# Twelve TensorE bodies for the expert widths in place of six

## The chip, the cores and the metric

One core of one Trainium2 chip runs the whole program in one launch. The metric is the device time of one execution in microseconds (us); three runs of the kernel before are given.

## The reference

One decoder layer on 1024 tokens of width 1024, all in f32: a mixer of latent attention and forgetting attention, a cross attention over 256 memory tokens, a mixture of 32 experts, and a last norm. Only the experts matter here:

```python
logits = (xt @ w_router).astype(jnp.float32) + b_router.astype(jnp.float32)
top_vals, top_idx = lax.top_k(logits, TOP_K)          # TOP_K = 4
gates = jax.nn.softmax(top_vals, axis=-1)
...
h = lax.ragged_dot(xs, w_gate_up, group_sizes) + b_gate_up[e_sorted]
glu = jnp.minimum(h[:, ::2], SWIGLU_LIMIT)
lin = jnp.clip(h[:, 1::2], -SWIGLU_LIMIT, SWIGLU_LIMIT)
act = glu * jax.nn.sigmoid(SWIGLU_ALPHA * glu) * (lin + 1.0)
y = lax.ragged_dot(act, w_down, group_sizes) + b_down[e_sorted]
```

Each token goes to 4 of the 32 experts, 4096 rows in all. The reference's router, worked out on its own inputs, gives the experts these numbers of tokens, largest first: 199, 195, 180, 171, 156, 152, 145, 143, 140, 138, 135, 131, 130, and then nineteen experts of 125 down to 78.

## The kernel before

The program runs its stages one after the other: memory keys and values, the input projections, attention, cross attention and router, and from about 1070 us on the experts. Every engine has its own instruction stream; semaphores tie them together.

**The router's end.** The vector engine counts the tokens of each expert, ranks the experts by size, largest first (`order`, `ahead_of`, `at_place`), and compares each expert's size with a row of widths (`widths`, filled by one memset for each width at L2231, compared at L2262 into `over_b`). A product with ones (L1724) turns that into `bounds`: how many experts are larger than 208, than 184, and so on. `items` holds, in rank order, the expert and its number of tokens.

**One item is one expert.** SyncE loads its weights into six slots of 2 MB (four of `w_gate_up`, two of `w_down`), GpSimd gathers its tokens' rows into `xg`, TensorE transposes them into `xe_t` (with VectorE), makes gate and up (`e_gate_up`: 128 products of 128x128 weights with w columns, L1376), VectorE and ScalarE make the activation over all 256 columns whatever w is, and TensorE makes the down product (`down`: 64 products with w columns, L1804). An f32 product stands in the trace as two matmul records, so an item has 256 records of L1376 and 128 of L1804. In between TensorE does parts of its neighbours: the index product and the gathered rows of the next item, and the rows of the item before on their way out. The body for w = 128 is another one: its down product takes the activations as weights (`e_rows_down`, L1836).

**The width is in the code, not in a register.** For each width from the largest down TensorE has a body of its own, inside five nested loops of two rounds; each level asks first whether the item counter `at` is still below the class's bound:

```python
def up_to(end, w, level):                 # L1914
    with pe.Fori(0, 2):                   # L1916
        with pe.If_lt(at, end):           # L1917
            if level == 1:
                item(w)
            else:
                up_to(end, w, level - 1)

for c, w in enumerate(reversed(WIDTHS)):  # L1923
    up_to(below[c], w, LEVELS)            # LEVELS = 5
```

The bounds are read into registers one by one ahead of that (`pe.value_load(bounds[...])`, L1886), the first three before `e_index(0)`, which makes the first item's gather indices, the others behind it; then come the transposes of the bias rows (L1892). A class whose bound is equal to the one before it is empty: TensorE asks at the outermost level, jumps over the body, goes round once more, and jumps over it again. Where a class ends in the middle of its loops, each level not yet finished asks once more and is refused. The other engines have one body for all widths, so nothing in their order depends on the class. Behind the classes stands one more body, for experts beyond 256 tokens (`further_blocks`, tested at L552), which this input does not use.

Of the kernel before, what the change touches and what calls it, by code (L numbers as in the profile page):

```python
# [30 lines left out]
P = 128  # L31
# [22 lines left out]
def shapes(x, mem, w_q_up, w_router, w_in):  # L54

    class S:
        pass

    S.T, S.D = x.shape[1:]
    S.NT, S.KD = S.T // P, S.D // P  # L60
    S.M = mem.shape[1]
    S.MT = S.M // P
    S.QR, S.KR, S.RO = 256, 128, 32
    S.H, S.DN, S.DV = 8, 64, 64
    S.DQ = S.DN + S.RO
    S.FW = S.H * S.DV
    S.LAT = S.QR + S.KR + S.RO + S.H
    S.IN = S.LAT + 3 * S.FW
    S.XH, S.XD = 4, S.D // 4
    S.E = w_router.shape[-1]  # L70
    S.TOP = 4
    S.CAP = 256
    S.MORE = S.T * S.TOP // (S.CAP + 1)
    S.ITEMS = S.E + S.MORE
    S.CLASSES = 6
    return S


def build(nc, S, a, out):
    T, D, NT, KD, H, FW, E, CAP = S.T, S.D, S.NT, S.KD, S.H, S.FW, S.E, S.CAP  # L80
    ctx = ExitStack()
    with ctx:
# [182 lines left out]
        widths = r("widths", [P, S.CLASSES - 1])  # L265
        over_b = r("over_b", [P, S.CLASSES - 1], BF16)

        WIDTHS = [P, 144, 160, 184, 208, CAP]
        assert len(WIDTHS) == S.CLASSES
        SLOTS = 6  # L270
        slots = [Region(95 + 16 * c, 111 + 16 * c)(f"slot{c}", [P, KD, 512]) for c in range(SLOTS)]
# [1093 lines left out]
        def _(pe):  # L1365
# [548 lines left out]
# [10 lines that stand above are left out]
                up_to(below[c], w, LEVELS)  # L1924
# [10 lines left out]
        def _(ve):  # L1935
# [294 lines left out]
            for c in range(S.CLASSES - 1):  # L2230
                ve.memset(widths[:, c:c + 1], float(WIDTHS[S.CLASSES - 2 - c]))  # L2231
            ve.wait_ge(c_rstd, 2)
# [295 lines left out]
```

## Time and profile before

| | us |
|---|---|
| runs | 2705.48, 2710.2, 2710.97; median 2710.2 |
| profiled execution, from its first to its last instruction | 2705.4 |
| experts, from the first gate product to TensorE's last | 1090.6 to 2689.2 |
| items at 208, 184, 160, 144, 128 columns | 2, 2, 3, 6, 19 |

The profile gives the span of its execution and no time of that execution beside it; the fastest run is 0.1 us above the span, the median 4.8 us. On the page an engine's share of busy time is one line, below it the span in 40 slices. "PE" is TensorE's matmul side, "PEld" its weight load, "PEldq" TensorE's sequencer, which handles loops, branches and register loads and hands matmuls to the engine's queue; its instructions are not counted as busy time, but a query by source line shows them.

### The profile page before, as it was taken

What the parts mean: (1) busy time and instruction counts of PE and PEld (TensorE: products, weight loads), DVE (VectorE), ACT (ScalarE), POOL (GpSimd) and SP (SyncE); (2) the same over time, 40 slices, a digit from 0 to 9 for tenths busy, and PEclk for the clock granted to TensorE, in tenths of its full rate; (3) what the DMA queues carried; (4) which work ended last, traced back from release to release, by engine and by line L of the source; (5) the groups of instructions that cost most, each with busy time, mean ns of one, the idle gap of its engine ahead of it and who ended that gap; (6) DMA issues with size and microseconds to landing.
All of it is one profiled execution on the core that took longest, in us unless ns stands there. A gap on an engine that the chain in (4) does not pass through costs nothing.

```text
span 2705.4 us, 49571 instructions
## 1 busy us (share of the span) xinstructions
PE 2638.0 (98%) x17206; PEld 2118.7 (78%) x17207; DVE 1091.5 (40%) x2701; ACT 627.4 (23%) x1386; POOL 379.9 (14%) x391
## 2 busy tenths in 40 slices
PE   9999999999999998999999999999999999999997
PEld 8455556666477774999999999998878787878785
DVE  1111145554212324433333344344455454545455
ACT  0333355553011112011111111111212121221212
POOL 0100022221000001111111111111111111112111
PEclk9999999999999998999999999999999999999998
DMA  8111243232300002765667677787888888888885
GB/s 293 47 51 54 64 151 90 79 116 92 129 1 9 31 31 103 303 209 194 221 218 254 225 276 260 269 274 264 318 299 319 301 310 306 312 297 312 300 310 202
DMA packets 108856, 533.95 MB, mean 197 GB/s; under 512 B 24290, under 2 KB 59042, under 8 KB 84208
## 3 DMA queue, kind: packets, MB, share of 16 engines
q1 hardware_dynamic: 88016, 498.99, 50.2%
q0 software_dynamic: 20768, 33.97, 5.7%
q8 instruction: 48, 0.79, 0.1%
q14 instruction: 24, 0.20, 0.0%
HBM read 506.64 MB, written 60.52 MB: 210 GB/s over the span
## 4 chain that ended last, share of the span: by engine, by line
PE 92%; DVE 3%; issue 2%; DMA 2%; ACT 1%; DVEq 1%; POOL 0%; ACTq 0%; POOLq 0%
PE bank L1376 45%; PE wide L1376 9%; PE wide L1836 9%; PE wide L1804 9%; PE bank L1426 8%; PE bank L1369 4%; PE wide L1500 2%; PE bank L1556 2%; PE bank L1760 2%; PE wide L1517 1%; DMA d_sum<-y_sb,sidx 1%; PE wide L1369 1%; DVE biased L2060 1%; DVE prob_t L2071 1%; ACT prob L1151 0%
## 5 line engine op out<-in xcount | busy, mean ns | idle before, releaser
L1376 PE MATMUL bank<-xe_t,slot 128*128 128x128 f32 (+4 forms) x8192 | 1025.2, 287 | 12.3 <-issue 11.2
L1376 PEld LDWEIGHTS bank<-xe_t,slot 128*128 128x128 f32 x8192 | 1014.5, 192 | 14.1 <-issue 13.7
L2336 DVE TENSOR_SCALAR glu<-bank,b_gu 128x256 f32<-128x256 f32 x256 | 123.8, 484 | 657.2 <-PE bank L1376 657.1
L1317 ACT ACTIVATE sig<-glu 128x256 f32<-128x256 f32 x256 | 106.7, 417 | 837.8 <-DVE glu L2336 835.5
L1836 PE MATMUL wide<-slot,act_t 128*128 128x512 f32 x608 | 267.8, 593 | 1.0 <-DVE act_t L2348 1.0
L1804 PE MATMUL wide<-act_t,slot 128*128 128x144 f32 (+3 forms) x1664 | 235.5, 302 | 0.0
L1804 PEld LDWEIGHTS wide<-act_t,slot 128*128 128x128 f32 x1664 | 231.8, 190 | 0.0
L1426 PE MATMUL bank<-w_in,xt 128*128 128x512 f32 (+1 forms) x512 | 217.6, 575 | 1.6 <-DVEq L1978 1.6
L1836 PEld LDWEIGHTS wide<-slot,act_t 128*128 128x128 f32 x608 | 112.5, 190 | 128.8 <-issue 126.2
L1334 ACT ACTIVATE y_t<-wide,b_dn 128x256 f32<-128x256 f32 x248 | 102.0, 471 | 421.2 <-PE wide L1836 212.9
L955 POOL DMA_INDIRECT xg<-d_xn,gidx x66 | 66.6, 1009 | 862.8 <-DVE gidx L2290 814.0
L1426 PEld LDWEIGHTS bank<-w_in,xt 128*128 128x128 f32 x512 | 94.8, 190 | 100.5 <-issue 100.5
L987 POOL DMA_INDIRECT share<-d_gate,sidx x64 | 67.8, 1059 | 458.6 <-DVEq L2357 415.4
L2348 DVE TENSOR_TENSOR act_t<-lin,sig 128x256 f32<-128x256 f32 x256 | 108.8, 425 | 41.0 <-issue 7.3
L1938 DVE TENSOR_TENSOR xe_t<-bank,gains 128x512 f32<-128x512 f32 x132 | 85.2, 686 | 96.8 <-PE bank L1760 91.6
L2338 DVE TENSOR_SCALAR lin<-bank,b_gu 128x256 f32<-128x256 f32 x256 | 121.6, 475 | 0.0
L2345 DVE TENSOR_TENSOR lin<-lin,glu 128x256 f32<-128x256 f32 x256 | 108.9, 425 | 19.4 <-issue 0.3
L1376 PEld LDWEIGHTS bank<-hn_t,w_xq 128*128 128x128 f32 x1024 | 115.5, 192 | 1.4 <-issue 1.1
L1376 PE MATMUL bank<-hn_t,w_xq 128*128 128x128 f32 x1024 | 115.7, 275 | 0.3 <-issue 0.3
L1376 PE MATMUL wide<-vw,px_t 128*128 128x512 f32 x256 | 112.4, 593 | 0.6 <-DVE lg_now L2171 0.6
L997 POOL DMA_INDIRECT d_sum<-y_sb,sidx x62 | 99.0, 1598 | 44.3 <-ACTq L1299 29.4
L1369 PE MATMUL bank<-const,prob 128*128 128x128 f32 x576 | 88.2, 281 | 11.6 <-DVE prob_t L2071 5.1
(302 smaller groups left out, 2455.6 us busy)
## 6 DMA issues: line engine op xcount, KB each, us to landing
slot<-in_w_gu SPq DMA_DIRECT2D x128, 2048.0 KB, 8.8
slot<-in_w_dn SPq DMA_DIRECT2D x64, 2048.0 KB, 7.7
w_in<-in_w_in SPq DMA_DIRECT2D x1, 6144.0 KB, 25.3
w_mem_k<-in_w_mem_kv SPq DMA_DIRECT2D x4, 1024.0 KB, 11.0
w_mem_v<-in_w_mem_kv SPq DMA_DIRECT2D x1, 4096.0 KB, 20.6
x_sb<-in_x SPq DMA_DIRECT2D x8, 512.0 KB, 3.3
cneg<-d_cneg SPq DMA_DIRECT2D x8, 512.0 KB, 6.6
d_vw<-mix_out SPq DMA_DIRECT2D x16, 256.0 KB, 2.2
```

The source lines that it names most:

```text
L997: po.indirect_dma_start(out=d_sum, out_offset=bass.IndirectOffsetOnAxis(ap=sidx[:, hb:hb + 1], axis=0), in_=y_sb[:, hb, :], in_offset=None ...
L1317: ac.activation(sig[m % 2][:, :], glu[m % 2][:, :], ACT.Sigmoid, scale=1.702).then_inc(e_sig, 1)
L1334: x = ac.activation(y_t[:, m, :], pp2[b][:, (m % 2) * CAP:(m % 2 + 1) * CAP], ACT.Identity, bias=b_dn[:, bass.ds(e * KD + m, 1)])
L1369: m = pe.transpose(dst[0:s.shape[-1], j * P:j * P + s.shape[0]], s, idn)
L1376: m = pe.matmul(dst, l, r_, start=(k == 0), stop=(k == n - 1))
L1426: m = pe.matmul(pp[b][:, 0:c1 - c0], xt[:, kk, :], w_in[:, kk, c0:c1], start=kk == 0, stop=kk == KD - 1)
L1804: x = pe.matmul(pp2[b][:, (m % 2) * CAP:(m % 2) * CAP + w], slots[4 + m // 4][:, k, (m % 4) * P:(m % 4 + 1) * P], act_t[:, k, 0:w], start= ...
L1836: x = pe.matmul(wide[1][:, hd * 512:(hd + 1) * 512], act_t[:, k, 0:P], slots[4 + hd][:, k, :], start=k == 0, stop=False)
L2336: ve.tensor_scalar(glu[b][:, :], pp[b][:, 0:CAP], b_gu[:, bass.ds(e * 2 * KD + 2 * m, 1)], 7.0, ALU.add, ALU.min).then_inc(e_glu, 1)
L2338: ve.tensor_scalar(lin[b][:, :], pp[b][:, CAP:2 * CAP], b_gu[:, bass.ds(e * 2 * KD + 2 * m + 1, 1)], 7.0, ALU.add, ALU.min).then_inc(e_gu[ ...
L2345: ve.tensor_tensor(lin[b][:, :], lin[b][:, :], glu[b][:, :], ALU.mult)
L2348: ve.tensor_tensor(act_t[:, m, :], lin[b][:, :], sig[b][:, :], ALU.mult).then_inc(e_act, 1)
```

## The change

The table of widths becomes every eighth number from 128 to 208, and 256: twelve classes and twelve bodies instead of six. Everything that depends on the number of classes follows: eleven memsets of `widths`, eleven columns in `over_b` and in its product, eleven bounds and eleven register loads. What a body does is unchanged.

```diff
@@ -72,7 +72,8 @@
     S.CAP = 256
     S.MORE = S.T * S.TOP // (S.CAP + 1)
     S.ITEMS = S.E + S.MORE
-    S.CLASSES = 6
+    S.STEP = 8
+    S.CLASSES = (208 - P) // S.STEP + 2
     return S
@@ -265,7 +266,7 @@
         widths = r("widths", [P, S.CLASSES - 1])
         over_b = r("over_b", [P, S.CLASSES - 1], BF16)
 
-        WIDTHS = [P, 144, 160, 184, 208, CAP]
+        WIDTHS = [*range(P, 208 + S.STEP, S.STEP), CAP]
         assert len(WIDTHS) == S.CLASSES
```

One line is added ahead of the bodies, so a line of TensorE's code has a number higher by one in the changed kernel (L1377 for L1376).

With the sizes above the experts fall into these classes:

| tokens | 199, 195 | 180 | 171 | 156 | 152 | 145 | 143, 140, 138 | 135, 131, 130 | the other 19 |
|---|---|---|---|---|---|---|---|---|---|
| width before | 208 | 184 | 184 | 160 | 160 | 160 | 144 | 144 | 128 |
| width after | 200 | 184 | 176 | 160 | 152 | 152 | 144 | 136 | 128 |

Summed over the 32 experts the columns fall from 4560 to 4496. Before, one class is empty (256). After, four are: 256, 208, 192 and 168.

TensorE, ahead of the first item. Before, from the first item's index product on (`mv`, `hot`) to the first test of class 256:

```order
L1376 MATMUL bank<-mv,hot 128x2 x16
L1886 TENSOR_LOAD bounds
L1886 ISA x2
...
L1892 MATMUL wide<-const,b_thrice 96x128 x8
L1916 UNCONDITIONAL_BRANCH
L1917 COMPARE_AND_BRANCH
```

and in the changed kernel:

```order
L1377 MATMUL bank<-mv,hot 128x2 x16
L1887 TENSOR_LOAD bounds
L1887 ISA x2
...
L1893 MATMUL wide<-const,b_thrice 96x128 x8
L1917 UNCONDITIONAL_BRANCH
L1918 COMPARE_AND_BRANCH
```

The load and its two further instructions stand twice before and eight times after between the index product and the bias rows; ahead of the index product they stand three times in both.

TensorE, the way from the last product of the body for 184 columns to the first of the next body, before:

```order
L1804 MATMUL wide<-act_t,slot_189 128x184 x16
L1917 UNCONDITIONAL_BRANCH
L1916 REGISTER_ALU
L1916 COMPARE_AND_BRANCH
...
L1909 COMPARE_AND_BRANCH
L1760 MATMUL bank<-const,xg 128x128 x16
...
L1376 MATMUL bank<-xe_t,slot_184 128x160 x16
```

and in the changed kernel the way from the body for 176 columns to the one that follows in the code:

```order
L1805 MATMUL wide<-act_t,slot_189 128x176 x16
L1918 UNCONDITIONAL_BRANCH
L1917 REGISTER_ALU
L1917 COMPARE_AND_BRANCH
...
L1910 COMPARE_AND_BRANCH
L1761 MATMUL bank<-const,xg 128x128 x16
...
L1377 MATMUL bank<-xe_t,slot_184 128x168 x16
```

The loop's ends and heads are the same (five of each), but what follows the body for 176 is a whole body for 168 columns, which no expert of this input enters, and only behind that the one for 160.

## Rows read from the trace of the kernel before

**Rows 1.** The page: span and busy time of the engines.
```profile
span 2705.4 us, 49571 instructions
PE 2638.0 (98%) x17206; PEld 2118.7 (78%) x17207; DVE 1091.5 (40%) x2701; ACT 627.4 (23%) x1386; POOL 379.9 (14%) x391
```

**Rows 2.** Groups by shape, L1376: line engine op, count | busy us, mean ns | idle before.
```profile
L1376 PE MATMUL bank<-xe_t,slot 128*128 128x128 f32 x4864 | 551.0, 275 | 2.7 <-issue 2.7
L1376 PE MATMUL bank<-xe_t,slot 128*128 128x144 f32 x1536 | 193.0, 288 | 3.3 <-issue 3.3
L1376 PE MATMUL bank<-xe_t,slot 128*128 128x160 f32 x768 | 105.9, 299 | 2.9 <-issue 2.9
L1376 PE MATMUL bank<-xe_t,slot 128*128 128x208 f32 x512 | 92.7, 344 | 1.0 <-DVEq L2305 1.0
L1376 PE MATMUL bank<-xe_t,slot 128*128 128x184 f32 x512 | 82.5, 324 | 2.4 <-issue 2.4
```

**Rows 3.** Timeline of TensorE: start, us, what, count, idle time before it.
```profile
1216.71 17.05 PE L1804 MATMUL wide<-act_t,slot 128*128 128x208 f32 x96
1236.15 11.91 PE L1376 MATMUL bank<-xe_t,slot 128*128 128x184 f32 x64 [2.39 <-issue]
...
1301.71 10.14 PE L1376 MATMUL bank<-xe_t,slot 128*128 128x184 f32 x64
...
1350.53 15.12 PE L1804 MATMUL wide<-act_t,slot 128*128 128x184 f32 x96
1368.52 8.96 PE L1376 MATMUL bank<-xe_t,slot 128*128 128x160 f32 x64 [2.87 <-issue]
...
1424.72 8.86 PE L1376 MATMUL bank<-xe_t,slot 128*128 128x160 f32 x64
...
1540.37 9.78 PE L1376 MATMUL bank<-xe_t,slot 128*128 128x144 f32 x64 [3.28 <-issue]
...
1593.13 8.00 PE L1376 MATMUL bank<-xe_t,slot 128*128 128x144 f32 x64
...
1850.02 7.41 PE L1376 MATMUL bank<-xe_t,slot 128*128 128x128 f32 x64 [2.70 <-issue]
```

**Rows 4.** TensorE's sequencer by source line: count: ns min/median/max, first and last start.
```profile
L1917 PEldq COMPARE_BRANCH  x92: 65/73/4747, 1078.5 to 2685.5; - x92
...
L1886 PEldq TENSOR_LOAD <-bounds x5: 295/306/309, 1074.8 to 1077.5; - x5
...
L552 PEldq COMPARE_BRANCH  x1: 4821/4821/4821, 2687.2 to 2687.2; - x1
```

**Rows 5.** The same by window: 1078 to 1084.3 (two rows), then 1231 to 1234.
```profile
L1917 PEldq COMPARE_BRANCH  x2: 221/2484/4747, 1078.5 to 1083.7; - x2
...
L1916 PEldq MOVE  x2: 35/36/38, 1078.4 to 1084.3; - x2
...
L1917 PEldq COMPARE_BRANCH  x4: 214/214/222, 1231.1 to 1233.8; - x4
```

**Rows 6.** The chain that ended last, 1080 to 1086: start, us, what.
```profile
1080.68 4.70 DMA xg<-d_xn,gidx
1085.37 0.39 issue
```

**Rows 7.** Windows: PE, PEld, DVE, ACT, POOL busy (count); PEclk, DMA share, GB/s.
```profile
1090.00:1094.00 4.00, 3.39 (x10) 3.31 (x11) 3.14 (x4) 0.00 (x0) 3.39 (x3) 0.50 1.00 426
1238.00:1242.00 4.00, 4.00 (x19) 4.00 (x18) 0.00 (x0) 0.00 (x0) 0.00 (x0) 0.65 0.77 328
1366.00:1372.00 6.00, 3.48 (x25) 3.49 (x26) 0.00 (x0) 0.63 (x2) 0.00 (x0) 1.00 0.82 298
```

**Rows 8.** DMA packets that fetch instructions, 1236 to 1540, then 1855 to 2680: count, MB, share.
```profile
q8 instruction: 7, 0.11, 0.2%
...
q8 instruction: 2, 0.03, 0.0%
```

## The prediction

> **What bounds the kernel now.** I read the page first, then the groups by shape, then TensorE's timeline over the experts, and last its sequencer, because the change adds nothing but code. The page shows TensorE's matmuls busy for 98% of the span and every other engine below half of it [rows 1]. So what counts is TensorE's time for an item, and whether it gets its next item at once.
>
> Per matmul record, the groups give 551.0/4864 = 0.113 us at 128 columns, 0.126 at 144, 0.138 at 160, 0.161 at 184 and 0.181 at 208 [rows 2]: the time follows the columns. Of 32 groups' starts only five have idle time ahead of them in these rows. One is the very first item, behind VectorE. The other four stand exactly where the width changes: 2.39, 2.87, 3.28 and 2.70 us, and what they wait for is "issue", that is, nothing that another engine owes [rows 2, 3]. Between two items of one width there is no gap. A change of width is therefore a cost of its own, 11.24 us in all, and the change makes more of them.
>
> There is a second cost behind it. The first 64 gate records after a change took 11.91 us at 184 columns, against 10.14 one item later; 9.78 against 8.00 at 144; but 8.96 against 8.86 at 160 [rows 3]. The granted clock says why: 0.65 in the four microseconds after the gap at 1236, which is a part at the lower level, 1.2 GHz, after an engine that had stood idle for 2.39 us; 1.00 around the gap of 2.87 us at 1368 [rows 7]. So two of four gaps brought the lower clock, at 1.77 us each.
>
> **What the sequencer shows.** The tests of line 1917 take 65 to 73 ns in the median and once 4747 ns [rows 4]. That one, at 1078.5, is the first jump over the body for 256 columns, which is empty. The second jump over the same body, on the loop's second round, took 221 ns [rows 5]. At the end of a class, four refused tests jump over a body that has just run, in 214 to 222 ns each [rows 5]. The jump over the last, unused body at the program's end took 4821 ns [rows 4]. So it is not the jump that is dear, and not its length, but landing in code that was not reached before. Instruction packets fit: seven of 16 KB while the classes of 184 and 160 made their first passes, and two in 825 us of the 128-column items [rows 8]. Seven packets for two bodies is about 56 KB for a body, and a body once run is kept. The Trainium skill, page "Runtime: NRT & Kernel Launch", section "Instruction fetch mechanics", says that a taken branch to a target outside what is held forces a fetch before execution goes on; it gives no time for it. By that rule the trace's two long branches are fetches; the trace agrees, and the time is the trace's.
>
> **The change, part by part.**
>
> *Fewer columns.* 4560 becomes 4496, 64 less. A down group of 96 records takes 17.05 us at 208 and 15.12 at 184 [rows 3]: 1.93/24 = 0.0804 us per column, times four for the 384 records of an item = 0.322 us per column and item. 64 x 0.322 = **-20.6 us**. No expert moves to or from the special body for 128 (the smallest above 128 has 130), so nothing else is saved. All of it lies on the path: TensorE has no gaps inside items. VectorE and ScalarE work on 256 columns in both and are under half busy. An item of 136 columns is still longer than one of 128, and those run without waiting for weights [rows 2], so weights don't become the bound.
>
> *Six more register loads.* Five loads start from 1074.8 to 1077.5 [rows 4], 0.68 us apart: six more take 4.1 us. What could cover them is the first item's gather. It lands at 1080.68 + 4.70 = 1085.38, and the transposes start 0.38 later [rows 6]. But the sequencer is no earlier: its walk through the empty class ends with the MOVE at 1084.3 [rows 5], and behind that stand the inner loop heads, four pairs of some 0.2 us and the two tests of the item, until about 1085.6. There is no slack left, so all of it is on the path: **+4.1 us**. If the gather were still the later one by half a microsecond, it would be 3.6; that is the low end. The bias rows behind the loads are used only at 128 columns, hundreds of microseconds later.
>
> *The empty class 208, ahead of the first item.* An empty class costs from one outer MOVE to the next, 1078.4 to 1084.3 [rows 5]: 5.9 us, of which 4.75 is the first jump. Before, one stands there (256), now two: **+5.9 us**. Low end: 1.1 us, if the target's code were already there. High end: the trace has only 4747 and 4821 ns, each once, so I allow half as much again, 7 us for the jump.
>
> *Changes of width.* Before, four. Now seven: 200 to 184 (across the empty 192), 184 to 176, 176 to 160 (across the empty 168), 160 to 152, 152 to 144, 144 to 136, 136 to 128. A gap has two parts that differ. Each level that isn't finished asks once more: after six items three times (gap 2.70), after two or three items four times (2.39 to 3.28), so after one item five times. The 144 class (three refusals, 2.70) against the 160 class (four, 3.28) makes a refusal 0.6 us. And the narrower the class that ends, the less work waits in TensorE's queue to cover it: 2.39 after 208, 2.87 after 184, 3.28 after 160, at four refusals each. So: 184 to 176, 2.87 + 0.6 = 3.5; 160 to 152, 3.28 + 0.6 = 3.9; 152 to 144, 3.3; 144 to 136, 3.4; 136 to 128, 3.5. The two across an empty class take 5.9 more: 200 to 184, 2.5 + 5.9 = 8.4; 176 to 160, 2.9 + 0.6 + 5.9 = 9.4. Sum 35.4, less the 11.2 of before: **+24.2 us**. Low end 14.7 (jumps already fetched), high end 28.
>
> *The clock.* Two of four gaps up to 3.28 us brought the lower clock. All seven are now 3.3 us or more. I take both long ones and four of the five short ones: 6 x 1.77 = 10.6, less 3.5 of before: **+7.1 us**. Bounds: -3.5 (no drop at all) and +12.4 (each of seven, the long ones for twice as long, since after the long idle ahead of the first item the clock was 0.50 for the whole stretch from 1090 to 1094 [rows 7]). The Trainium skill's page "TensorE: Matmul & The Clock Gate", section "HAM oscillation", says that the loss is paid again at every idle stretch that is long enough; by that rule all seven lose it, 12.4 in place of 10.6, and the sum would be 1.8 higher.
>
> *The rest.* Six memsets of `widths` and six more columns in one compare and one product come to under half a microsecond; the memsets stand in front of a wait of VectorE for the next stage, which covers them. If they were not covered, 0.4 us.
>
> Sum: -20.6 + 4.1 + 5.9 + 24.2 + 7.1 = **+20.7 us** on the profiled execution's span of 2705.4 us, so 2726.1. That execution is at the low end of the runs, whose median is 4.8 us above it; against the median it is 2710.2 + 20.7 = 2730.9, rounded to **2731**.
>
> **The rivals.** A measurement of this kernel can tell 0.2%, 5.4 us, from no change.
>
> *A. The forecast*, 2731, its own range 2722 to 2740 by the bounds above. Chance 0.70.
>
> *B. Empty bodies cost no fetch.* The three new empty classes are crossed at 1.1 us each instead of 5.9, say because short classes leave the fetcher ahead. 3 x 4.8 = 14.4 less: 2716.5. For it: one of the jumps of before was into cold code right after another stage, so it may have been dear for that. Against it: the 4821 ns at the end. The page "Advanced Engine Details and Errata" of the Trainium skill, section "Control Flow Timing", gives about 108 ns for a compare-and-branch, which agrees with the 65 to 222 ns here but not with the two long ones; by it alone B would hold. Chance 0.12, just above the 0.2% in half of it.
>
> *C. The columns win.* B's cheap jumps, and the clock stays up at the gaps, since it did at 2.87 us. Then -20.6 + 4.1 + 1.1 + 14.7 - 3.5 = -4.2, and if the gather covers the start after all, -9.4: 2701. It decides where all that is added stays under 15.2 us (20.6 - 5.4). Nothing in the rows gives both at once. Chance 0.05.
>
> *D. Thin classes fall behind the fetcher.* Three classes now hold a single item, so their body runs once and the next one must have been fetched during that pass; before, each had two passes or more. If entering after a single pass stalls for 4.75 us, three of these add 14: 2745. For it: bodies are kept only after a first pass. Against it: the packets of a first pass come during that pass, with 50 us to spare. Chance 0.11.
>
> *E. Nothing is done.* The classes might not be chosen as I counted (a size off by a few tokens); then some of the terms shrink together. Chance 0.02, about no change.
>
> Faster 0.05 (C). Within 0.2%: part of B and E, 0.07. Slower 0.88. The range from 2715 to 2743 takes in A with its bounds and B, and leaves out C, D and E.
>
> **What would show it.** In the changed profile: matmul groups at 200, 176, 152 and 136 columns with 512, 256, 512 and 768 records of L1377, and none at 208; on line 1918 four branches of 4 us or more (before the first item two, two among the items) where there was one; seven gaps "issue" ahead of L1377, two of them above 8 us; the first gate product some 10 us later than 1090.6; the clock below 1.00 behind most gaps; and the 128-column items as long as before, 44 us. The prediction is wrong if the crossings of 192 and 168 show branches of 0.2 us (then B), if entries after single items show long branches (D), or if the first gate product starts where it did.

## The result, and the profile after

The changed kernel takes 2743.4 us (median of four runs, 2739.1 to 2746.1) against 2709.1 of before: a ratio of 1.0128, 95% interval 1.0113 to 1.0142. It is slower, as forecast, but by 34 us where 21 were forecast, and lies just outside the range. One execution of this study, of the kernel with nine widths in nested loops, took 5527.5 us, twice as long as any other; it counts in that kernel's median and not in its ratio.

The groups by shape (columns as in [rows 2]) show that the table of widths does what it says: records at 200, 176, 152 and 136 columns in the numbers foretold, and none at 208.

```profile
L1377 PE MATMUL bank<-xe_t,slot 128*128 128x128 f32 x4864 | 552.7, 276 | 3.8 <-issue 3.8
L1377 PE MATMUL bank<-xe_t,slot 128*128 128x144 f32 x768 | 97.3, 289 | 3.2 <-issue 3.2
L1377 PE MATMUL bank<-xe_t,slot 128*128 128x136 f32 x768 | 92.1, 282 | 3.4 <-issue 3.4
L1377 PE MATMUL bank<-xe_t,slot 128*128 128x200 f32 x512 | 89.3, 337 | 1.0 <-DVEq L2306 1.0
L1377 PE MATMUL bank<-xe_t,slot 128*128 128x152 f32 x512 | 68.9, 297 | 3.8 <-issue 3.8
L1377 PE MATMUL bank<-xe_t,slot 128*128 128x184 f32 x256 | 42.2, 328 | 12.0 <-issue 12.0
L1377 PE MATMUL bank<-xe_t,slot 128*128 128x176 f32 x256 | 41.7, 328 | 3.4 <-issue 3.4
L1377 PE MATMUL bank<-xe_t,slot 128*128 128x160 f32 x256 | 38.0, 313 | 18.2 <-issue 18.2
```

The idle times put down to "issue" at the rows' ends are the seven gaps. TensorE's timeline (as [rows 3]) has them in order of time, with the first group after each:

```profile
1224.86 16.41 PE L1805 MATMUL wide<-act_t,slot 128*128 128x200 f32 x96
1253.29 11.93 PE L1377 MATMUL bank<-xe_t,slot 128*128 128x184 f32 x64 [12.03 <-issue]
...
1322.45 12.74 PE L1377 MATMUL bank<-xe_t,slot 128*128 128x176 f32 x64 [3.42 <-issue]
...
1405.07 11.54 PE L1377 MATMUL bank<-xe_t,slot 128*128 128x160 f32 x64 [18.20 <-issue]
...
1523.10 8.43 PE L1377 MATMUL bank<-xe_t,slot 128*128 128x152 f32 x64
1580.05 9.77 PE L1377 MATMUL bank<-xe_t,slot 128*128 128x144 f32 x64 [3.24 <-issue]
```

Among the items TensorE stands idle 47.9 us, in seven gaps, where it stood 11.2. The five direct changes of width cost 3.2 to 3.8 us each, the two across an empty class 12.0 and 18.2. The sequencer's branches of line 1918 (line 1917 before, [rows 4, 5]), in windows around 1083.7, 1089.2, 1242.4, 1388.6 and 1395.5 us, say what happens there:

```profile
L1918 PEldq COMPARE_BRANCH  x1: 4484/4484/4484, 1083.7 to 1083.7; - x1
...
L1918 PEldq COMPARE_BRANCH  x1: 6619/6619/6619, 1089.2 to 1089.2; - x1
...
L1918 PEldq COMPARE_BRANCH  x1: 7190/7190/7190, 1242.4 to 1242.4; - x1
...
L1918 PEldq COMPARE_BRANCH  x1: 6176/6176/6176, 1388.6 to 1388.6; - x1
...
L1918 PEldq COMPARE_BRANCH  x1: 7384/7384/7384, 1395.5 to 1395.5; - x1
```

In order these are the jumps over 256, 208, 192, 168 and, the one that nobody had on the list, 168 once more, on the loop's second round. At the other empty classes the second jump took 0.22 us. In the trace of the changed kernel every one of the five has an instruction packet of queue q8 that starts 2.3 to 2.5 us before the branch ends. A shorter stall stands on line 1910 ahead of the item of 184, 1.1 us.

The chain that ended last shows the start (as [rows 6]): the gather lands at 1081.80 + 5.04 and the transposes start 11.53 us later, where 0.39 stood before.

```profile
1081.80 5.04 DMA xg<-d_xn,gidx
1086.83 11.53 issue
```

And the clock over 20 us around the longest gap (as [rows 7]) is at the lower level (0.50, which is 1.2 GHz) throughout, with TensorE idle for most of it:

```profile
1390.00:1410.00 20.00, 4.93 (x18) 4.94 (x19) 0.00 (x0) 0.00 (x0) 0.00 (x0) 0.50 0.23 90
```

**Where 38.9 us went**, from span 2705.4 to span 2744.3 (the profiled execution of the changed kernel is its slowest, 2746.1 us, so this is 4 to 5 us more than the medians differ by). The start is taken from the first item's index product to its first gate product (13.8 us before, 25.1 after); the clock is each first group of 64 records less the same group one item later, or, where there is one item, less 64 records at the pace of the width.

| term | forecast | measured |
|---|---|---|
| 64 columns less | -20.6 | -20.6 |
| start: six loads and the crossing of 208 | +10.0 | +11.3 |
| gaps among the items | +24.2 | 47.86 - 11.24 = +36.6 |
| clock behind them | +7.1 | 14.4 - 3.8 = +10.6 |
| before the experts | 0 | +1.3 |
| sum | +20.7 | +39.2 |

The sum is 0.3 us above the difference of the spans. The 1.3 us ahead of the experts come and go from run to run: the first index product starts between 1076.7 and 1080.4 us in the profiles of this study.

### The profile page after: what moved, and what is told of

Same layout as the page of the kernel before. It is cut to its first block, busy times and chain, and to the rows that moved or that the text cites. A ratio compares the mean times of both kernels' runs of the same rounds, so it can differ in the third digit from the quotient of the medians.

```text
span 2744.3 us, 49707 instructions
## 1 busy us (share of the span) xinstructions
PE 2628.9 (96%) x17206; PEld 2108.8 (77%) x17207; DVE 1090.2 (40%) x2707; ACT 627.9 (23%) x1386; POOL 380.6 (14%) x391
## 4 chain that ended last, share of the span: by engine, by line
PE 91%; issue 3%; DVE 3%; DMA 1%; ACT 1%; DVEq 1%; ACTq 0%; POOL 0%; POOLq 0%
PE bank L1377 45%; PE wide L1377 9%; PE wide L1837 9%; PE wide L1805 8%; PE bank L1427 8%; PE bank L1370 4%; PE wide L1501 2%; PE bank L1557 2%; PE bank L1761 2%; PE wide L1518 1%; PE wide L1370 1%; DVE biased L2061 1%; DMA d_sum<-y_sb,sidx 1%; DVE prob_t L2072 1%; ACT prob L1152 0%
## 5 line engine op out<-in xcount | busy, mean ns | idle before, releaser
L1377 PE MATMUL bank<-xe_t,slot 128*128 128x128 f32 (+7 forms) x8192 | 1022.1, 287 | 48.9 <-issue 47.9
L1377 PEld LDWEIGHTS bank<-xe_t,slot 128*128 128x128 f32 x8192 | 1011.4, 193 | 51.2 <-issue 51.0
L1805 PE MATMUL wide<-act_t,slot 128*128 128x144 f32 (+6 forms) x1664 | 228.6, 298 | 0.0
L1805 PEld LDWEIGHTS wide<-act_t,slot 128*128 128x128 f32 x1664 | 225.2, 190 | 0.0
L1377 PEld LDWEIGHTS bank<-hn_t,w_xq 128*128 128x128 f32 x1024 | 115.5, 192 | 1.4 <-issue 1.1
L1377 PE MATMUL bank<-hn_t,w_xq 128*128 128x128 f32 x1024 | 115.7, 275 | 0.3 <-issue 0.3
L1377 PE MATMUL wide<-vw,px_t 128*128 128x512 f32 x256 | 112.4, 593 | 0.6 <-DVE lg_now L2172 0.6
## 6 DMA issues: line engine op xcount, KB each, us to landing
w_in<-in_w_in SPq DMA_DIRECT2D x1, 6144.0 KB, 25.1
```

Of the source, the lines that this page charges most:

```text
L1377: m = pe.matmul(dst, l, r_, start=(k == 0), stop=(k == n - 1))
L1805: x = pe.matmul(pp2[b][:, (m % 2) * CAP:(m % 2) * CAP + w], slots[4 + m // 4][:, k, (m % 4) * P:(m % 4 + 1) * P], act_t[:, k, 0:w], start= ...
```

## Experiments

Theory 1: the cost is made of two things, the sequencer's walk through the nested loops at each change of width, and a stall of several microseconds whenever it lands behind a body that has not run. The main rival: it is the number of bodies and changes that costs, and empty ones are cheap.

**Empty classes alone.** Before's widths, and three more that no expert falls into.

```diff
-    S.CLASSES = 6
+    S.CLASSES = 9
-        WIDTHS = [P, 144, 160, 184, 208, CAP]
+        WIDTHS = [P, 144, 160, 168, 184, 192, 208, 232, CAP]
```

> Before's six widths and three more, 168, 192 and 232, into which no expert of this input falls: every item runs at the width of before. Theory 1 (landing behind a whole body that was not yet run costs a fetch of instructions): three new crossings. Ahead of the first item 2.0 us for three register loads and 6 to 8 us for the body of 232; the gap from 208 to 184 grows from 2.4 to 11 to 13 us and the one from 184 to 160 from 2.9 to between 12 and 19 us; the clock costs 2 to 5 us more: in all 25 to 40 us slower than before. Theory 2 (what costs is changing between bodies that run, and an empty class costs its five instructions): 2.0 + 3 x 1.1 = 5 us slower, all branches of line 1917 under 0.3 us but the first.

Measured: 2749.0 against 2707.8 us, ratio 1.0147 (1.0130 to 1.0164), 40 us slower with no item changed; theory 2 is out. The branches around the empty classes 192 and 168 (two rows, each with the shortest, the mean of two and the longest):

```profile
L1917 PEldq COMPARE_BRANCH  x2: 3435/6802/10170, 1242.4 to 1246.4; - x2
...
L1917 PEldq COMPARE_BRANCH  x2: 6544/6841/7138, 1392.2 to 1399.9; - x2
```

Here both rounds stall at both classes (3.4 and 10.2, 7.1 and 6.5 us), and the gaps are 18.7 and 17.5 us. Ahead of the first item the new class costs less: the first gate product comes 6.8 us later after its index product than before, three register loads included.

**Empty classes with short bodies.** The same, with eight products as the body of an empty class.

```diff
             def item(w):
+                if w in (168, 192, 232):
+                    product(pp[0][:, 0:w], [(slots[0][:, k, 0:P], xe_t[:, k, 0:w]) for k in range(KD)])
+                    pe.reg_mov(at, pe.snap(at) + 1)
+                    return
```

> As e_empty, but the bodies of the three empty classes hold eight products in place of a whole item; no expert enters them, so nothing of the computation is left out. Theory 1a (the stall is for blocks of code that are not held, so it needs a body longer than what is fetched ahead): the crossings of 232, 192 and 168 cost about 1.1 us each, no branch over 1 us but the one over the whole body of 256; 5 us slower than before. Theory 1b (landing behind any code that was not run stalls, whatever its length): branches of 4 to 7 us at all three, 25 to 40 us slower, as e_empty.

Measured: 2716.1, ratio 1.0027 (1.0017 to 1.0037), 7 us slower. All 98 branches of the test's line:

```profile
L1921 PEldq COMPARE_BRANCH  x98: 65/75/4839, 1083.6 to 2696.0; - x98
```

The one at 4839 ns is the whole body of 256; no other of these was long, and the gaps ahead of 184 and 160 are 3.7 and 4.0 us, 1.2 more than before. So landing behind code that did not run brings no stall when that code is short; it takes a long body. The Trainium skill (page "Runtime: NRT & Kernel Launch", section "Instruction fetch mechanics") says that a taken branch whose target lies outside the code held at that moment has to wait for a fetch. This run agrees: the long body brings a stall and the short one does not. What is held at the moment of a jump no trace shows.

**The same items without the empty classes.**

```diff
-    S.CLASSES = 6
+    S.CLASSES = 9
-        WIDTHS = [P, 144, 160, 184, 208, CAP]
+        WIDTHS = [P, 136, 144, 152, 160, 176, 184, 200, CAP]
```

> The changed table without the three empty widths: 128, 136, 144, 152, 160, 176, 184, 200, 256. The same items at the same widths as in the changed kernel, 4496 columns. Theory 1: no stalled branch but the one over 256; -20.6 us of columns, +2.0 of loads, seven gaps of 2.4 to 3.9 us (23.6 less 11.2 = +12.4), the clock lost at all seven (12.3 less 3.7 = +8.6): +2 us, 2711. Theory 2 (the number of changes of width and of bodies is what costs): 15 us or more slower than before, with gaps as in the changed kernel.

Measured: 2712.8 against 2707.8, ratio 1.0013 (1.0003 to 1.0023). TensorE's waits among the items:

```profile
PE bank L1376 <- issue: 23.8, 7, 3.8
```

Seven gaps, 23.8 us, 23.6 foretold. With 4496 columns, as the changed kernel, and some 30 us faster than it, each against its runs of before: the three empty classes are nearly all of its loss, and what is left of the columns' 20.6 us goes to the walks and the clock.

**One jump in place of two.**

```diff
             for c, w in enumerate(reversed(WIDTHS)):
-                up_to(below[c], w, LEVELS)
+                with pe.If_lt(at, below[c]):
+                    up_to(below[c], w, LEVELS)
```

> The changed kernel with one more test of the item counter around each class's five loops, so an empty class is jumped over once and not twice. Theory 1 with the second jump's stall being due to the jump back (which fetches from the loop's start again and gives up the block just landed in): the 7.4 us branch ahead of 160 is gone, each of the four crossings loses about 1 us more, the extra test costs 0.3 us at eight full classes; the first jumps still stall for 4.5 to 7 us: 2733, 10 us faster than the changed kernel. Rival (a crossing needs two fetches in any case, the second merely showed on the second jump): about 2742, with a stalled branch elsewhere, ahead of 160.

Measured: 2733.3, ratio 1.0091 (1.0070 to 1.0111), some 9 us faster than the changed kernel, each against its runs of before. First jumps of 5.4, 5.2 and 6.4 us remain at 208, 192 and 168, and the two long gaps are 10.1 and 10.2 us. No long branch has taken the place of the second one ahead of 160, so the second stall at 168 belonged to going round the loop. Ahead of 184 a branch inside the item (line 1910) took 2.2 us, where it took 1.1 in the changed kernel: there part of the stall has only moved.

**Is a stall's length a matter of the code or of the moment?** The changed kernel again, and then with some 128 instructions more in the body of 256, which nobody enters.

> The changed kernel once more, unchanged, for a second profile. If the stalls follow from the code alone, the branches at 208, 192 and 168 (two) come out within 1 us of 6.6, 7.2, 6.2 and 7.4 us; if from what the transfers do at that moment, they scatter by 2 us or more.

Measured: 2746.6 us in its one run, and the branches at 192 and 168 (first and second jump; the 214 ns in the middle row is a refused test just before):

```profile
L1918 PEldq COMPARE_BRANCH  x1: 7407/7407/7407, 1244.4 to 1244.4; - x1
L1918 PEldq COMPARE_BRANCH  x2: 214/3185/6156, 1390.1 to 1390.7; - x2
L1918 PEldq COMPARE_BRANCH  x1: 7412/7412/7412, 1397.6 to 1397.6; - x1
```

7.41, 6.16 and 7.41 us, against 7.19, 6.18 and 7.38. The lengths repeat. The traffic repeats as well (81 and 79% of the DMA engines busy during the jump at 192), so this alone does not say that the code decides. Other traces say that the traffic does not: the first jump at 192 in the kernel with empty classes took 3.4 us at 79%, and the second jump at 168 in the changed kernel 7.4 us at 4% (columns as in [rows 7], in this order):

```profile
1242.40:1245.80 3.40, 0.00 (x0) 0.00 (x0) 0.00 (x0) 0.30 (x1) 0.00 (x0) 1.00 0.79 224
...
1395.50:1402.90 7.40, 0.00 (x0) 0.00 (x0) 0.00 (x0) 0.00 (x0) 0.00 (x0) 0.50 0.04 7
```

The next run changes the code alone.

```diff
             def item(w):
+                if w == CAP:
+                    product(pp[0][:, 0:w], [(slots[0][:, k % KD, 0:P], xe_t[:, k % KD, 0:w]) for k in range(32)])
```

> The changed kernel, with 32 more products in the body for 256 columns, which no expert enters: all code behind it lies some 128 instructions, half a 16 KB packet, further on. Nothing else changes. Theory 1b (where the bodies lie against the fetched blocks decides how long a crossing stalls and whether the second jump stalls too): the three stalled branches among the items change in length and the second jump's stall moves or goes; 3 to 12 us either way from the changed kernel. Rival (the state after single passes decides, 176 having run once): the branches at 192 and 168 keep their lengths within 1 us, the second stall stays at 168, and the time is within 4 us of the changed kernel.

Measured: 2737.0, ratio 1.0097 (1.0081 to 1.0112), some 6 to 8 us faster than the changed kernel, by medians and by ratios. ("Theory 1b" is here the one about where the code lies, not that of the short bodies.) The branches from 1240 on (192 twice, then 168; the 214 and 221 ns are refused tests just before):

```profile
L1920 PEldq COMPARE_BRANCH  x2: 214/2344/4474, 1240.4 to 1241.0; - x2
L1920 PEldq COMPARE_BRANCH  x1: 9288/9288/9288, 1246.1 to 1246.1; - x1
L1920 PEldq COMPARE_BRANCH  x2: 221/3478/6734, 1392.1 to 1392.7; - x2
```

The second stall has moved from 168 to 192. So where the code lies changes both the lengths and the place of the second stall, and that class 176 has run only once does not set them. That it is the place within a 16 KB packet that counts is a reading; only this one shift was tried.

**Six more register loads alone.**

```diff
+            for c in range(6):
+                pe.value_load(bounds[0:1, c % 5:c % 5 + 1], min_val=0, max_val=E)
             below.append(E)
             pe.wait_ge(r_ex, 3)
```

> Before's six widths with six more register loads of bounds (their values unused) where the changed kernel has its six. Theory 1 (no slack at the start): the first gate product comes 4 us later against the index product of the first item, and the time is 3.9 us longer. Rival (the gather covers them): within 1 us of before.

Measured: 2711.7 against 2708.5, ratio 1.0010 (1.0001 to 1.0019), 2.7 us; the interval reaches from 0.3 to 5.1 us, so the time alone does not rule the rival out. The trace does. From the index product to the first gate product it is 17.1 us (1076.69 to 1093.75) instead of 13.8, 3.3 more. The loads are not covered; 0.7 us of their 3.9 came back because the jump over 256 behind them took 4.04 us instead of 4.75.

**A price list put to use.** Seven classes, none empty but 256.

```diff
-        WIDTHS = [P, 144, 160, 184, 208, CAP]
+        WIDTHS = [P, 136, 144, 160, 184, 200, CAP]
```

> Nested loops as before; 208 becomes 200, and 136 is added: 128, 136, 144, 160, 184, 200, 256. No class but 256 is empty. By the prices measured (0.322 us for a column of an item, 3.4 for a gap, 1.75 for the clock, 0.65 for a load): -12.9 for 40 columns (16 at 200, 24 at 136), +3.4 +1.75 +0.65: 7 us faster than before. Rival (a change of width costs twice that, as the changed kernel's totals would give if spread over its changes): within 2 us of before.

Measured: 2705.3 against 2707.3, ratio 0.9988 (0.9979 to 0.9997), 3 us faster, not 7: a miss. The gaps sum to 15.5 us, 0.9 more than foretold, and the clock fell behind all five, also behind those of 2.51 and 2.91 us, where I had counted three. From the profile: -12.9 for the columns, +4.3 for gaps, +5.1 for the clock, which with 0.65 for the load makes -2.9 in all. The length of such a gap does not say whether the clock falls: of before's, it fell behind 2.39 us and not behind 2.87.

**The walk taken away.** One test and one loop with its bound in a register, in place of five nested loops.

```diff
             def up_to(end, w, level):
-                with pe.Fori(0, 2):
-                    with pe.If_lt(at, end):
-                        if level == 1:
-                            item(w)
-                        else:
-                            up_to(end, w, level - 1)
+                with pe.If_lt(at, end):
+                    with pe.Fori(pe.snap(at), end):
+                        item(w)
```

With six widths:

> Before's six widths; the five nested loops of two rounds around each body become one test and one loop that runs from the item counter to the class's bound. Theory 1 (the gap at a change of width is the sequencer's walk through refused tests and loop heads, 5.1 to 5.9 us of which TensorE's queue covers 2.3 to 3.3): the walk is about 1.2 us and fits under the queue, all four gaps (11.2 us) and the clock lost behind two of them (3.6) go: 15 us faster than before. Rival (the gap is for entering new code, whatever the loops): gaps of 2 us or more stay, within 4 us of before.

Measured: 2692.3 against 2707.3, ratio 0.9949 (0.9934 to 0.9965), 14 us faster. No gap is left at a change of width:

```profile
1163.13 11.42 PE L1376 MATMUL bank<-xe_t,slot 128*128 128x208 f32 x64
1234.59 10.14 PE L1376 MATMUL bank<-xe_t,slot 128*128 128x184 f32 x64
```

With the nine widths in use:

> The same loop with the nine widths that this input fills (128, 136, 144, 152, 160, 176, 184, 200, 256). Theory 1: the 64 columns are saved at no gap and no lost clock: -20.6 + 2.0 for loads - 11.2 - 3.7 = 33 us faster than before, 2675, and 36 us faster than the same nine widths in nested loops. Rival (entering a body after a single pass finds its code missing): gaps stay ahead of 176, 160 and 152.

Measured: 2673.1, ratio 0.9871 (0.9856 to 0.9887), 35 us faster than before and 38 to 40 us faster than the same widths in nested loops, by ratios and by medians. There is no gap at a change of width and no lower clock among the items, also not behind the single items of 184, 176 and 160; the granted clock is 1.00 from 1110 to 1900 us:

```profile
1232.43 10.14 PE L1376 MATMUL bank<-xe_t,slot 128*128 128x184 f32 x64
1296.21 9.71 PE L1376 MATMUL bank<-xe_t,slot 128*128 128x176 f32 x64
1357.43 8.86 PE L1376 MATMUL bank<-xe_t,slot 128*128 128x160 f32 x64
1413.54 8.43 PE L1376 MATMUL bank<-xe_t,slot 128*128 128x152 f32 x64
```

With the changed kernel's twelve:

> The changed kernel's twelve widths in the same single loop: every empty class is jumped over once, with no walk. Theory 1: what is left of the change's cost is the fetch at the first landing behind a body not run: 5 to 7 us each at 208, 192 and 168 (and 256, as before), of which TensorE's queue covers some 2 us at 192 and 168. Against the nine widths in the same loop 2.0 us of loads, 5.5 at the start, two gaps of 3 to 5 us and 3.5 us of clock: 17 to 21 us slower than those, 2692 to 2696. Rival (the landings were slow only because of the walk): within 4 us of the nine.

Measured: 2683.3, ratio 0.9918 (0.9902 to 0.9933), 22 us faster than before and 10 us slower than the nine, where 17 to 21 were expected. The stalls are there (3.9 us at 256, 5.3 at 208), but at 192 and 168 they are shorter, 3.5 and 3.9 us, and part of each is covered by what waits in TensorE's queue. TensorE's waits among the items, two gaps of 1.7 and 2.4 us with no lower clock behind them, where gaps of 3 to 5 us and 3.5 us of clock were expected:

```profile
PE bank L1377 <- issue: 4.1, 2, 2.4
```

## Why the prediction was right in sign and wrong in size

*What bounds the kernel:* right. TensorE's columns and its idle time between bodies are the whole account; the 128-column items take 44 us as before.

*Fewer columns:* right, 0.322 us for a column of an item. The nine widths in single loops against the six bear it out in measured time: 19.2 us apart, where 20.6 less 2.0 for three loads is 18.6.

*Six loads with no slack:* right, 3.3 us alone instead of 4.1.

*Direct changes of width:* right. 3.42, 3.77, 3.24, 3.37 and 3.83 us, where 3.5, 3.9, 3.3, 3.4 and 3.5 were written. Five refusals instead of four cost 0.55 and 0.49 us (3.42 against 2.87, 3.77 against 3.28), where 0.6 was written.

*The clock:* under-sized. 10.6 us instead of 7.1, within its bounds. All seven gaps lost it where six were counted, and the loss behind 176 and 160 was 3.0 and 2.7 us, more than 1.77, so that the seven sum to 14.4, where 10.6 was written for six (3.8 and 3.5 of before come off these). The prediction also weighed a rule of the Trainium skill (page "TensorE: Matmul & The Clock Gate", section "HAM oscillation"), that the loss is paid again at every idle stretch that is long enough; the trace agrees with it in the count of seven. But two of four was no bad reading either: the granted clock stayed at 1.00 behind a gap of 3.18 us ahead of 160 with the six loads, and behind one of 3.46 us ahead of 128 in the shifted kernel.

*The empty classes:* this is the step that failed. "An empty class costs from one outer MOVE to the next ...: 5.9 us, of which 4.75 is the first jump" was one sighting, ahead of the first item, and was set at 208, 192 and 168 alike, with 7 us as the high end of a jump and the second jump taken as free, because it was 0.22 us in that sighting. The mechanism held, the price didn't: the jumps took 6.6, 7.2 and 6.2 us, and 168 paid a second one of 7.4. The two gaps came to 12.0 and 18.2 us where 8.4 and 9.4 were written, 12.4 us too little, and with the clock behind them that is most of the miss; the term for changes of width, +36.6, lies above its own high end of 28. The trace of before could not show it: it had one crossing, and the runs show that the length depends on where the code lies (some 128 instructions of shift turned 7.2 + 0.2 and 6.2 + 7.4 into 4.5 + 9.3 and 6.7 us). A range for a stall seen once should have reached to twice its length. One reading behind the step was wrong as well: "not its length, but landing in code that was not reached before". The short bodies were not reached before either, and jumping over them took 0.2 us.

*The rivals:* B (no fetch) is ruled out by the five long branches, C with it, and E by the groups at the widths counted. D (single passes fall behind the fetcher) gives 2745 and is near the measured time, but is wrong: the changes after the single items of 184 and 160 stalled nowhere (3.42 and 3.77 us), and nine widths in single loops have no gap at all. Its time was right by chance.

*Left open:* why landing behind the same body takes 3.5 and 3.9 us at 192 and 168 in single loops and 7.2 and 6.2 in the changed kernel. The walk goes back and forth over the body just run ahead of the jump, and in the trace of the changed kernel the packet that ends the stall at 192 starts 4.8 us after the branch, not 1.0 as in the single loops; which of these jumps delays it was not tried. That the second stall at 168 comes from going round the loop is shown by its absence with one jump; what is given up in between is not.

## What to carry to other kernels

A table of specialised bodies costs by its entries, also by those that no input of the day uses: here 0.65 us for each bound loaded, and 5 to 16 us for each empty body jumped over in nested loops (2 to 4 in single ones), against 0.322 us saved for each column of an item. Look at what the sequencer does between two bodies before adding bodies: its walk and its branches count as no engine's busy time, and rewriting five nested loops as one gave 14 us with the six widths. It turned the twelve widths from 34 us slower than before into 22 faster, and the nine that this input fills from 3.5 slower into 35 faster. A cost seen once in a trace is one sighting and not yet a price: the same kind of jump took 3.4 to 10.2 us in these runs.

## What was not expected of the hardware

The second jump over a body can stall although the first has just landed at the same place (7.4, 10.2, 6.5 and 9.3 us in four profiles), and a shift by some 128 instructions moves it from one class to another. In two profiles of the same kernel the stalls' lengths agree within 0.25 us. Whether TensorE's clock falls behind a gap of 2.4 to 3.5 us does not follow from its length: it fell behind 2.39, 2.51 and 2.91 us and not behind 2.87, 3.18 and 3.46, and behind 2.70 us ahead of 128 it fell in one kernel and stayed up in another. Behind 1.7 and 2.4 us it did not fall.
